# A two-block transformer kernel: barriers between stages replaced by waits on single slots, and the modulation product made in fp32 on four column groups

## The reference, cut to what matters

```python
silu_c, silu_cc = silu(c), silu(c_ctx)
for l in range(2):
    mod_x = silu_c @ w_ada[l] + b_ada[l]           # 1024 -> 6144, six parts of 1024
    mod_c = silu_cc @ w_ada[l] + b_ada[l]
    hx = rms_norm(x, g1[l]) * (1 + sc1_x) + sh1_x  # the context the same way with its own parts
    q, k, v of three mixers = hx @ w_in[l]         # A: 8 heads, grouped; B: 4 heads, window with bias;
                                                   # C: 4 heads, difference of two softmaxes
    x = x + gt1_x * (concat(oa, ob, oc) @ w_out[l])
    x = x + gt2_x * (conv_ffn(modulated norm of x))
    # in layer 0 the context is updated by the same steps, with keys of the context alone
```

## Time and profile before

| | |
|---|---|
| median of 3 runs | 3846.23 us (3844.26 to 3849.02) |
| the profiled execution | 3845.96 us, of which the span of the trace is 3844.0 us |
| PE busy | 3587.7 us, 93% |
| DVE, ACT, POOL busy | 1780.4, 1623.8, 1651.4 us |
| mean granted TensorE clock | 0.955 |
| moved by DMA | 355.55 MB, 92 GB/s over the span |

### The profile page before, as it was taken

How to read it: one execution, slowest core, us unless ns; L and a number is a source line. 1 busy time by engine, 2 the same in 40 slices (tenths; PEclk the granted TensorE clock), 3 DMA queues, 4 the chain that set the end, 5 groups by cost and what they waited for, 6 DMA issues and landing times.

```text
span 3844.0 us, 49821 instructions
## 1 busy us (share of the span) xinstructions
PE 3587.7 (93%) x19478; PEld 2836.8 (74%) x19478; DVE 1780.4 (46%) x2946; ACT 1623.8 (42%) x2660; POOL 1651.4 (43%) x1066
## 2 busy tenths in 40 slices
PE   6999877999999899879999999999999999989998
PEld 4765555788899776557888666977887667878886
DVE  6754644442243674744362386353114476252114
ACT  5446645442355437633433235434222334443222
POOL 2644331444478644313444352524444442524442
PEclk8999987999999899989999999999999999999998
DMA  8433220333356622203333321412332221413331
GB/s 248 119 94 99 89 69 27 103 99 93 93 154 176 146 82 89 88 28 96 99 94 93 75 72 39 132 50 83 95 97 77 74 61 50 126 45 93 98 94 60
DMA packets 642464, 355.55 MB, mean 92 GB/s; under 512 B 70469, under 2 KB 614841, under 8 KB 642233
## 3 DMA queue, kind: packets, MB, share of 16 engines
q1 hardware_dynamic: 630451, 339.67, 31.4%
q10 hardware_dynamic: 11782, 12.71, 1.1%
HBM read 346.28 MB, written 6.05 MB: 92 GB/s over the span
## 4 chain that ended last, share of the span: by engine, by line
PE 84%; DVE 8%; ACT 3%; issue 2%; DMA 1%; POOL 1%; ACTq 0%; DVEq 0%; SPq 0%
PE psum L848 67%; PE psum L1007 5%; PE psum L1031 3%; PE psum L1049 2%; ACT work L1405 1%; PE psum L924 1%; DVE neg_max L1827 1%; PE psum L1078 1%; PE psum L956 1%; PE psum L887 1%; PE psum L977 1%; PE psum L1056 1%; DVE work L1706 1%; PE psum L1211 1%; PE psum L880 1%
## 5 line engine op out<-in xcount | busy, mean ns | idle before, releaser
L826 POOL TENSOR_TENSOR w_lo<-w_raw,w_hi 128x1024 fp32r<-128x1024 f32 (+3 forms) x1016 | 1589.7, 1583 | 2097.2 <-ACT w_hi L1274 2096.9
L848 PE MATMUL psum<-h_hi,w_hi 128*128 128x512 f32 (+1 forms) x3024 | 1159.7, 383 | 66.3 <-DVEq L1666 29.5
L848 PE MATMUL psum<-h_lo,w_hi 128*128 128x512 f32 (+1 forms) x3024 | 1124.4, 372 | 0.0
L848 PE MATMUL psum<-h_hi,w_lo 128*128 128x512 f32 (+1 forms) x3024 | 1124.2, 372 | 0.0
L1274 ACT ACTIVATE w_hi<-w_raw 128x1024 fp32r<-128x1024 f32 (+1 forms) x626 | 655.1, 1047 | 721.4 <-PE psum L848 628.8
L848 PEld LDWEIGHTS psum<-h_hi,w_hi 128*128 128x128 f32 x3024 | 580.7, 192 | 212.0 <-issue 47.0
L848 PEld LDWEIGHTS psum<-h_lo,w_hi 128*128 128x128 f32 x3024 | 582.9, 193 | 99.8 <-issue 9.1
L848 PEld LDWEIGHTS psum<-h_hi,w_lo 128*128 128x128 f32 x3024 | 581.1, 192 | 96.9
L848 PE MATMUL psum<-hid_hi,w_hi 128*128 128x512 f32 (+1 forms) x1040 | 392.2, 377 | 2.0 <-POOL w_lo L826 2.0
L848 PE MATMUL psum<-hid_lo,w_hi 128*128 128x512 f32 (+1 forms) x1040 | 391.2, 376 | 0.0
L848 PE MATMUL psum<-hid_hi,w_lo 128*128 128x512 f32 (+1 forms) x1040 | 391.1, 376 | 0.0
(11 more groups left out here) (212 smaller groups left out, 3890.6 us busy)
## 6 DMA issues: line engine op xcount, KB each, us to landing
w_raw<-in_w_up_dram SPq DMA_DIRECT2D x132, 512.0 KB, 3.8
w_raw<-in_w_ff_dram SPq DMA_DIRECT2D x128, 512.0 KB, 4.0
w_raw<-in_w_in_dram SPq DMA_DIRECT2D x92, 512.0 KB, 3.8
w_raw<-in_w_ada_dram SPq DMA_DIRECT2D x80, 512.0 KB, 3.9
w_raw<-in_w_down_dram SPq DMA_DIRECT2D x48, 512.0 KB, 4.1
w_raw<-in_w_mkv_dram SPq DMA_DIRECT2D x32, 512.0 KB, 4.1
w_raw<-in_w_down_dram SPq DMA_DIRECT2D x24, 384.0 KB, 3.5
w_ada_first<-in_w_ada_dram SPq DMA_DIRECT2D x4, 2048.0 KB, 19.4
```

What stands on the lines that cost most here:

```text
L826: m = nc.gpsimd.tensor_tensor(WL[:, c % NSPLIT, k:k + step, :], RAW[:, c % NRAW, k:k + step, :], WH[:, c % NSPLIT, k:k + step, :].bitcast( ...
L848: m = pe.matmul(out_ap, lhs(a, k), rhs(b, k), start=(k == 0 and n == 0), stop=(k == nk - 1 and n == 2))
```

## The change

- No engine calls `stage_end` any more. The first tile of each output projection waits slot by slot for `o_lo` (or `cv_lo`) of the slot that it reads; the first tile of the mixer's input projection of block 2, layer 0, waits for `h_lo` slot by slot; each attention waits for the last copied tile and the last rotated tile before its scores, for the last value tile before its first transposes. The sum for the norm after `x`'s output projection is made after the second scores of the context's attention.
- The modulation is a plain fp32 product of the raw weight with the 2 silu columns stationary. Product k goes to output partitions 32 (k mod 4) and the next one, so that four follow each other on four column groups; the small product that turns the rows adds the four groups. ACT and POOL split no `w_ada`. The raw buffer is free when TensorE has used it.
- Chunks ride in pairs: in layer 0 in each of steps 0 to 11 and every second one up to 34, in layer 1 in every second step up to 30.
- The four blocks of the start are each one run of 8 such products, with the turning of `x` and the context between the first and second.
- SP issues the 21 rest rows before the fourth 2 MB transfer; the 14 gain rows go out on ACT's queue after the silu. The repeated bias is written after the context projection of layer 0.
- The rope tables stand behind tiles 8 to 11 of the context projection in layer 0 and 1 to 4 in layer 1, the bias tables behind tiles 8 to 15 of `x`'s projection; the window mask is added in steps 4 to 7 of the attention over `x`.

```diff
@@ ada_beside
-        return parts[2 * step:2 * step + 2] if step < 8 else parts[step + 8:step + 9]
-    return parts[step:step + 1]
+        pair = step if step < 12 else step // 2 + 6 if step % 2 == 0 else len(parts)
+    else:
+        pair = step // 2 if step % 2 == 0 else len(parts)
+    return parts[2 * pair:2 * pair + 2]
@@ SP
             for i in range(4):
                 if i == 3:
                     sp.wait_ge(*at("turned", "first_rows"))
-                    gain_rows()
+                    rest_of_rows()
                 sp.dma_start(WA[:, i, :, :], w).then_inc(*mark(f"ada_in{i}", "first", 16))
-            rest_of_rows()
-            tables = {IDS["qkv", "c", l][0] + TABLE_LAG + n: (l, n) for l in range(DEPTH) for n in range(12)}
+            tables = {IDS["qkv", "c", l][ROPE_LAG[l] + n]: (l, n) for l in range(DEPTH) for n in range(4)}
+            tables.update({IDS["qkv", "x", l][BIAS_LAG + n - 4]: (l, n) for l in range(DEPTH) for n in range(4, 12)})
                 if c >= NRAW:
-                    sp.wait_ge(*at("w_lo", c - NRAW))
+                    sp.wait_ge(*at("w_used" if CHUNKS[c - NRAW][0] == "w_ada" else "w_lo", c - NRAW))
@@ POOL
-                nk = KT if name == "w_ada" else nk
+                if name == "w_ada":
+                    continue
@@ TensorE
-            def stage_end():
-                stage[0] += 1
-                pe.drain().then_inc(*mark("stage_end", ("pe", stage[0])))
-                pe.wait_ge(sems["stage_end"], 3 * stage[0])
             def product(out_ap, lhs, rhs, nk, normed=None, amid=None, ready=None):
                 for k in range(nk):
+                    if ready is not None:
+                        pe.wait_ge(*ready(k))
-            def ada_product(out_ap, hi, lo, j):
-                for k in range(2):
-                    for n, w in enumerate((hi, lo)):
-                        m = pe.matmul(out_ap, SILUS[:, 2 * j + k, :], w[:, k, :], ...)
+            def ada_product(bank, w, nk, done, j, last):
+                for k in range(nk):
+                    g = 32 * (k + done) % P
+                    m = pe.matmul(PS[g:g + 2, bank, :], SILU[:, j + k, :], w(k), start=j + k < 4, stop=j + k >= last - 4)
@@ TensorE, ada
-                    hi, lo = weights(c)
+                    pe.wait_ge(*at(f"w_loaded{c % NRAW}", c))
+                    w = wide(RAW[:, c % NRAW])
+                    ada_product(7, lambda k: w[:, k, :], 2, 2 * j, 2 * j, KT).then_inc(*mark("w_used", c))
@@ TensorE, new: what the first tile of an output projection waits for
+            def out_ready(att):
+                S, groups = att["S"], att["groups"]
+                def ready(k):
+                    if S[0] == "att2" and k < 2:
+                        return at("cv_lo", (S[1], k))
+                    if S[0] == "att3":
+                        return at("o_lo", (S, len(groups) - 2 + k // 4))
+                    return at("o_lo", (S, [g["tile"] for g in groups].index(k)))
+                return ready
@@ TensorE, attentions of block 1
+                    if s == "x":
+                        attend(att, before=[at("raw_copied", (S, n - 1)), at("rope_step", (S, 12, "sum"))],
+                               before_turn=[at("v_copied", (S, n - 1))])
+                    else:
+                        attend(att, before=[at("resid", (("out", "x", l), KT - 1))],
+                               before_value=[at("tok_std", ("n2", "x", l))], beside=lambda: rms_stat(("n2", "x", l)))
+                    out_proj(("out", s, l), IDS["out", s, l], TOKENS[s], att)
@@ ACT, in the attention
-                        nc.scalar.activation(AROW[:, :], PS[0:4, 7, :], ACT.Copy)
+                        nc.scalar.activation(AROW[:, :], PS[:, 7, :], ACT.Copy)
-                    for l, b, j in ada_beside(S, i):
-                        split_ahead(IDS["ada", l, b, j][0])
+                    if att["one_out"] and len(steps) - 4 <= i < len(steps) - 4 + AHEAD:
+                        split(IDS["out", S[1], S[2]][i - len(steps) + 4])
@@ DVE, in the attention over x
+                    if S[:2] == ("att", "x") and 4 <= i < 4 + B_HEADS:
+                        ...
+                        nc.vector.tensor_tensor(TB[:, h], TB[:, h], WINDOW.unsqueeze(1).broadcast_to([P, 14, 64]), ALU.add)
```

257 lines of the change are left out of this document (115 added, 142 removed).

## The result

The changed kernel takes 3739.53 us (median of 4 runs, 3738.19 to 3745.92) against 3847.62 us for the kernel before, run beside it (3844.26 to 3849.05): a ratio of 0.9724, 95% interval 0.9707 to 0.974. That is 108 us less. I had forecast 73, and the range, 3746 to 3804, ended 6 us above what came.

A forecast was written before the change was run, and what follows sets the result against it. TensorE was taken as the bound, its unchanged dense tiles most of the chain. Terms -23.4 - 4.9 + 4 - 12 - 30 - 5 - 1.5 = -73 took 3845.96 to 3773 us; range 3746 to 3804.

The forecast's parts named there:

- the rivals: Two groups at a time 3793, 0.14; joints' wait replaced 3793 to 3800, 0.14; SP order 3786, 0.07; no overlap 3880, 0.04.
- a pair of chunks: Modulation in attention over x: four fp32 products on four column groups cost 1.2 us; 0.98 if four run at a time.
- layer 0, steps 0 to 15: Attention over x: 13 pair steps at 5.72 plus three group ends of 1.95 and others, 94.0 against 117.4, -23.4 us.
- layer 1, steps 0 to 15: Attention over x: seven pair steps at 5.72, others at 4.58, 87.1 against 92.0, -4.9 us.
- window add: Eight adds moved before the maxima of steps 4 to 7, 0.5 us each, +4 us.
- start: Modulation before the first dense tile: last block arrives at 47, then 9.3 instead of 21.4 us; -12 (-17 to -4).
- waits at barriers (idle time of TensorE): Removing 21 barriers with 38.8 us of TensorE waiting saves 30 us (-20 to -38).
- half clock behind them (the same work shorter): After the long joint TensorE ran 10.30 us at clock 0.51; shorter waits save 5 us (-14 to +3).
- tables: Tables out of layer 1's short context projection, where a wait of 1.80 stood behind weights on SP: -1.5 us (-3 to 0).
- The wait at the joints: After attention x, 21 products on slots 0 to 6 fill 5.0 of the 6.79 us wait, twice: -10 us.
- I set both equal: Start: SP's later issue of the last block and its faster landing without the pad write cancel; arrival at 47 (-5, +8).
- all bounds good: Good end of the range, 3746: every term at its favourable bound, halved.

The follow-up runs named there:

- the wait filled: Unread fp32 products in seven waits ahead of output projections, against the changed kernel with first tiles waiting for their last slot (3779.4): 3773.36 us.
- the early write: Changed kernel with the 3.8 MB repeated-bias write issued on ACT's queue before the last 2 MB block, against the changed kernel: 3750.67 us, 11.1 longer.
- the old order: Changed kernel with the 14 gain rows on SP ahead of the fourth block and the 21 others behind it, against the changed kernel: 3740.96 us.

## Why the prediction was wrong, point by point

The mechanisms were the forecast's, none of the rivals came, and one group of terms was mis-sized: the barriers with the clock, forecast at 35 us and measured at 61.7.

| step of the forecast | forecast | measured |
|---|---|---|
| a pair of chunks | 1.2 | 0.93 |
| layer 0, steps 0 to 15 | 94.0 | 93.8 |
| layer 1, steps 0 to 15 | 87.1 | 86.1 |
| steps 16 to 23, layers 0 and 1 | 0 (-3 to 3) | -0.7, +0.8 |
| steps 24 to 38 | 0 (-3 to 3) | +1.8, -2.2 |
| window add | +4 | 0 |
| start | -12 (-17 to -4) | -17.4 |
| waits at barriers (idle time of TensorE) | -30 (-20 to -38) | -42, of which 34 at the barriers |
| half clock behind them (the same work shorter) | -5 (-14 to +3) | -21 |
| barriers and clock together | -35 | -61.7 |
| tables | -1.5 | -1.5 |

**Barriers and half clock: the step that failed.** "-30 (-20 to -38)" for the waits was near: 34 us of waiting at the barriers went, 42 of idle time in all. "**-5** (-14 to +3)" for the clock was not: with the barriers back TensorE is busy 21.0 us longer with the same instructions. I took the term from one window behind one long joint (10.30 us at 0.51) and read it as the price of that joint. It should have been multiplied over the places: even waits of at most 0.8 us at the start of an attention went with a granted clock of 0.76 and 0.66. A bound was at hand: the kernel before had a mean clock of 0.955, 346 us at half, and if TensorE worked all through it, 173 us hung on it; I never wrote that sum down. What the runs showed in its place: 42 us of idle time went together with 21 us of slower work, four times the term. The windows behind the joints show the mechanism: 0.94 and 0.96 of the clock with a wait, 1.00 with the wait filled. The Trainium skill (TensorE: Matmul & The Clock Gate, HAM oscillation) says this of a kernel that waits on loads between groups of products: the array falls back, and the next group pays. The trace agrees, with waits on other engines.

**The wait at the joints**, 21 products over 5.0 us of a wait of 6.79 with 1.8 left, was right: 1.65 is left. That slot 7 is late next, by the normalisation on VectorE, is what the rows at 494.02 and 498.85 show. Against the kernel with the barriers back, where the tile starts 7.92 behind the start of the last spread and the projection lasts 46.20 at 0.94 of the clock, the change has 0.56 + 1.65 and 46.06 less 1.65, at 1.00: 5.7 us won by the parts, 1.8 by the clock of the tiles behind.

**Four column groups.** 1.2 was too high by 0.27, and 0.93 is under my lower bound of 0.98. In layer 0 the error had no effect on the sum, because another stood against it: blocks now come twice as often, and each needs a turning product that makes its step 6.32 instead of 5.53. 13 pairs at 0.27 are 3.5; four turnings more than the three that were in my group ends, at 0.79, 3.2. The Trainium skill's figure (TensorE: Matmul & The Clock Gate, Packing small matmuls), 2.38 times for three groups and by my estimate 3.17 for four, is below the 3.6 to 3.75 measured here. The other rule cited, a drain at a change of the tiling mode (TensorEngine Tiling (Array Packing), Key Properties), does not show: from the values at 298.15 to the narrow products is 1.46 us, as it was before the change, and the four take 0.97 with the way to the next transposes in it. What doesn't shrink with the number of groups is the 0.08 us above.

**Window add.** I charged 0.5 for each of eight adds because a maximum stands behind it. TensorE limits these steps, and 22.04 with the adds is 22.04 without.

**Start.** Two errors against each other. "I set both equal" was wrong by 7.0 us of landing (40.03 against 47.07): the write of 3.8 MB cost the block that, shown by the early write (17.6 us from issue to use, against 10.7). The way from there to the first tile was 11.0 and not 9.3: the products took 3.59 and not 3.0, and the tail 7.4 and not 6.3. The clock was 0.50 in all of it, and 0.78 in the last 6.70 us before the first tile of the kernel before, from which I took the tail. The order of the copies came out neutral, as forecast, but partly by luck: the forecast looked only at the block, and the old order holds back the first weight load by 7.65 us, which cancels what the earlier block wins.

**Tables.** In layer 1 the gap between the context's last product and x's first fell from 7.69 to 4.28 us; with the barriers back it was 5.23. The wait of 1.80 is 0.26 in both, so the tables gave the forecast 1.5. The other 0.9 of the 2.5 is the spreads in that gap, which took 1.16 us with the barriers back instead of 2.07.

The range was too narrow because its good end halved "all bounds good" in one sum. The bounds of the clock and the start were passed on the same side (21 against 14, 17.4 against 17), and so was that of the waits if all idle time is counted (42 against 38). Waits and clock hang together: a shorter wait can also give back clock.

## What to carry to other kernels

When barriers go, count what the waiting engine could do meanwhile, not the barrier: starting the next tile on the operands that are there was 40 of the 62 us. Price every TensorE wait with the clock behind it; one less the mean granted clock, times the span, bounds that, and here the clock added 21 us to 42 us of idle time. Compare busy times of the same instructions to see what it really cost. Small products belong in the steps in which another engine limits: the same products moved there brought another 25 us.

## What the runs showed of the hardware that I had not expected

- Four fp32 products of 512 columns with two stationary columns each, on four column groups, take 0.97 us together, one after the other on one group 3.52, on two groups 1.81.
- 21 barriers, with 34 us of waiting at them, cost 62 us: 42 of idle time and 21 of longer work at a lower clock. Five of seven projections behind a filled wait ran their 192 products at 1.00 of the clock instead of 0.91 to 0.97. Work that nobody reads made them 9 us shorter together, and the same idea made the context's attention 4.8 us longer.
- A 3.8 MB write (each row 64 times) in flight made a 2 MB load take 17.6 us instead of 10.7 from issue to use.
